# First norm: x turned once without its factor, the factor applied when products are read out; GpSimd splits seven weight units; head sums spaced evenly

## What is computed

```python
n = x * rsqrt(mean(x*x, -1) + eps) * g_mix                # x [512, 1024]
q, k, v, u, bg, cg, ga, gc = split(n @ w_in + b_in)       # 512 x6, 1024 x2
q, k = rms_norm per head of 64, times g_q, g_k
ya = chunked attention(q, k, v) with a bias by distance   # 8 heads
yc = bg * (conv_b + sum_j conv_w[j] * shift(cg * u, j))   # 3 taps
m = sigmoid(ga) * (ya @ w_pa) + sigmoid(gc) * (yc @ w_pc)
h = x + m @ w_o
```

## Time and profile before

| | |
|---|---|
| median of 3 runs | 1943.93 us (1943.56 to 1945.12) |
| the profiled execution | 1943.7 us, of which 1941.5 us from first to last instruction |
| PE busy | 1885.3 us, 97% of the span |
| DVE, ACT, POOL busy | 919.2, 637.9, 139.9 us |
| mean granted TensorE clock | 0.989 |

### The profile page before, as it was taken

The page is one execution under the profiler, slowest core; times in us unless marked ns, Lnnn a source line. Parts: engine busy times, 40 slices in busy tenths (PEclk is TensorE's granted clock), DMA queues, the critical chain, the costliest instruction groups (busy, mean ns, idle before and its releaser), DMA issues.

```text
span 1941.5 us, 31375 instructions
## 1 busy us (share of the span) xinstructions
PE 1885.3 (97%) x13564; PEld 1565.4 (81%) x13564; DVE 919.2 (47%) x1611; ACT 637.9 (33%) x1187; POOL 139.9 (7%) x120
## 2 busy tenths in 40 slices
PE   7999999999999989999899999999999999999998
PEld 6877788866666656669789999998967898888898
DVE  5766334233333333358863423348766564423355
ACT  6344323111111111136432222234466543222242
POOL 0022000110000000000000000005222000000011
PEclk9999999989999999999899999999999999999999
DMA  5222342789999999973112332334311213332343
GB/s 191 88 76 77 110 164 88 280 329 429 430 428 430 428 429 427 428 283 95 56 45 87 90 107 78 97 109 133 110 63 55 87 45 109 99 107 83 102 127 112
DMA packets 57149, 345.16 MB, mean 178 GB/s; under 512 B 7168, under 2 KB 7808, under 8 KB 44976
## 3 DMA queue, kind: packets, MB, share of 16 engines
q1 hardware_dynamic: 53184, 334.15, 46.3%
q0 software_dynamic: 3504, 8.54, 1.2%
q10 hardware_dynamic: 320, 0.43, 0.1%
HBM read 343.09 MB, written 4.19 MB: 179 GB/s over the span
## 4 chain that ended last, share of the span: by engine, by line
PE 87%; DVE 7%; DMA 4%; ACT 1%; issue 1%; POOL 1%; SPq 0%; DVEq 0%; POOLq 0%; ACTq 0%
PE bank L487 57%; PE bank L702 10%; PE bank L726 6%; DMA e<-in_we 3%; PE bank L737 1%; PE bank L738 1%; PE bank L543 1%; PE bank L1135 1%; DVE wlo L1319 1%; PE bank L689 1%; PE bank L919 1%; PE bank L1083 1%; PE bank L880 1%; PE bank L1055 1%; PE bank L560 1%
## 5 line engine op out<-in xcount | busy, mean ns | idle before, releaser
L1319 DVE TENSOR_TENSOR wlo<-raw,whi 128x1024 fp32r<-128x1024 f32 x230 | 288.4, 1261 | 127.2 <-ACT whi L2319 123.5
L2319 ACT CAST whi<-raw 128x1024 fp32r<-128x1024 f32 x231 | 239.8, 1043 | 123.6 <-PE bank L487 106.5
L702 PE MATMUL bank<-e,xT 128*64 128x256 f32 x2048 | 236.9, 385 | 1.1 <-DVE xT L1592 0.8
L702 PEld LDWEIGHTS bank<-e,xT 128*64 128x64 f32 x2048 | 143.6, 138 | 82.5 <-issue 13.0
L487 PE MATMUL bank<-nhi,whi 128*128 128x272 f32 (+1 forms) x672 | 191.6, 285 | 1.1 <-DVE sl L1848 0.6
L487 PE MATMUL bank<-nhi,wlo 128*128 128x272 f32 (+1 forms) x672 | 191.2, 285 | 0.0
L487 PE MATMUL bank<-nlo,whi 128*128 128x272 f32 (+1 forms) x672 | 190.6, 284 | 0.0
L487 PE MATMUL bank<-n1hi,whi 128*128 128x512 f32 (+1 forms) x448 | 162.6, 363 | 0.0
L487 PE MATMUL bank<-n1lo,whi 128*128 128x512 f32 (+1 forms) x448 | 160.7, 359 | 0.0
L487 PE MATMUL bank<-n1hi,wlo 128*128 128x512 f32 (+1 forms) x448 | 160.7, 359 | 0.0
L487 PEld LDWEIGHTS bank<-nhi,whi 128*128 128x128 f32 x672 | 127.2, 189 | 2.0 <-DVE sl L1848 0.8
(11 more groups left out here) (397 smaller groups left out, 3767.9 us busy)
## 6 DMA issues: line engine op xcount, KB each, us to landing
e<-in_we SPq DMA_DIRECT2D x94, 2048.0 KB, 21.2
raw<-in_w_down SPq DMA_DIRECT2D x64, 512.0 KB, 3.5
raw<-in_w_gate SPq DMA_DIRECT2D x44, 512.0 KB, 3.5
raw<-in_w_up SPq DMA_DIRECT2D x44, 512.0 KB, 3.5
raw<-in_w_q SPq DMA_DIRECT2D x12, 512.0 KB, 4.3
B<-in_rel POOLq DMA_DIRECT2D x8, 512.0 KB, 4.9
raw<-in_w_gc SPq DMA_DIRECT2D x8, 512.0 KB, 3.5
raw<-in_w_ga SPq DMA_DIRECT2D x8, 512.0 KB, 4.2
```

What stands on the lines that cost most here:

```text
L702: p = e.matmul(b[64 * hf:64 * hf + 64, 0:256], x[:, k, :], W[:, k, 256 * hf:256 * hf + 256], start=(k == 0), stop=(k == 7))
L1319: e.tensor_tensor(wlo[wslot(u)][:], raw[u % NRAW][:], whi[wslot(u)][:].bitcast(F32), ALU.subtract).then_inc(*hit("dve_low", ("lo", u)))
L2319: e.copy(whi[wslot(u)][:], raw[u % NRAW][:]).then_inc(*hit("act_high", ("hi", u)))
```

## The change

- **Start.** x is turned as it comes. `xhi` and `xlo` are made from the unscaled x. The turned banks are also copied into `hT` (k = 0 and 4 to 7 by ScalarE, 1 to 3 by VectorE), and only that copy frees a bank. `pe_raw_x` goes. SyncE issues weight unit 0 ahead of x. ScalarE casts unit 0 first, squares three tiles, then runs xhi 0, xhi 1, copy 0, xhi 2, xhi 3, the cast of unit 1, xhi 4 to 7, the fourth square, copies 4 to 7.
- **Factor.** The roots are laid on a diagonal (`dg`, one VectorE multiply of two tensors in SBUF). Four fp32 matmuls of ones with it spread them over the partitions (`pe_spread_x`, step 12, in tile q 1), and ScalarE copies them to `rb`.
- **Readout.** Each of q, k, cg, u, bg, gc, ga is multiplied by `rb` on VectorE first: 8 + 12 + 8 + 8 multiplies. For q, k, cg, gc, ga this frees the bank, and ScalarE's bias or sigmoid then works in SBUF. u and bg are multiplied in their bank. V takes the root as the scalar of its one instruction.
- **Units 1 to 7** have their low part made by GpSimd.
- **Head sums** come one per tile: `HEAD_LAG` is 3 for the first and 6 for the others.

The core of the diff:

```diff
+    POOL_LOW = range(1, 8)
...
-                w.wait_ge(*at("xr", i))
+                w.wait_ge(*at("x", i))
...
+        def pe_spread_x():
+            b = take(("rb x",), SIDE)
+            w.wait_ge(*at("diag x"))
+            for i in range(4):
+                p = e.matmul(b[:, i * 128:(i + 1) * 128], ones, dg[:, i, :], start=True, stop=True)
...
-        side.add(nothing(3))
+        side.add(nothing(8))
         side.add(pe_meta())
-        side.add(pe_raw_x(range(6)))
+        side.add(nothing(2))
+        side.add(pe_spread_x())
...
-    HEAD_LAG = 2
+    HEAD_LAG = (3,) + 7 * (6,)
...
         def dve_load():
...
             feed(0)
+            root_x(0)
             for k in range(8):
                 w.wait_ge(*at("x hi", k))
                 e.scalar_tensor_tensor(xlo[:, k, :], bk("x", k), v1("g_mix", k), xhi[:, k, :].bitcast(F32), ALU.mult,
-                                       ALU.subtract).then_inc(*hit("dve_norm", ("xn", k), ("free", "x", k)))
+                                       ALU.subtract).then_inc(*hit("dve_norm", ("xn", k)))
+            for k in (1, 2, 3):
+                e.tensor_copy(hT[:, k, MT:L], bk("x", k)).then_inc(*hit("dve_out", ("free", "x", k)))
+            root_x(2)
+            w.wait_ge(*at("root", "x", 0))
+            w.wait_ge(*at("root", "x", 2))
+            e.tensor_tensor(dg[:], ident.unsqueeze(1).to_broadcast([128, 4, 128]),
+                            xs[:, 0, 0:4].unsqueeze(2).to_broadcast([128, 4, 128]), ALU.mult).then_inc(
+                                *hit("dve_norm", ("diag x",)))
+
+        def x_scaled(to, *key):
+            w.wait_ge(*at("free", "rb x"))
+            w.wait_ge(*at("out", *key))
+            e.tensor_tensor(to, bk(*key, 0), rb[:, 0:S], ALU.mult).then_inc(*hit("dve_out", ("free", *key, 0)))
+
+        def x_scaled_there(*key):
+            w.wait_ge(*at("free", "rb x"))
+            w.wait_ge(*at("out", *key))
+            e.tensor_tensor(bk(*key, 0), bk(*key, 0), rb[:, 0:S], ALU.mult).then_inc(*hit("dve_out"))
+            w.wait_ge(*last("dve_out"))
...
                 tile(J["bg", i], 0, at_k={1: first, 3: lambda: tap(1), 5: lambda: tap(2)})
+                x_scaled_there("bg", i)
...
         def dve_branches():
...
+                tile(J["gc", h], 0, at_k={CONV_LAG: lambda: conv_low(3)} if h == 0 else {})
+                tile(J["gc", h], 1, at_k={1: lambda: gate(0)})
                 for m in range(2):
                     k = 2 * h + m
-                    tile(J["pc", h], m)
-                    w.wait_ge(*at("free", "gc", k, 0))
+                    tile(J["pc", h], m, at_k={} if m else {1: lambda: gate(1)})
+                    w.wait_ge(*at("gate c", k))
...
         for i in range(8):
             tile(J["q" if i < 4 else "k"], i % 4)
-            side.add(nothing(HEAD_LAG))
+            for j in (0, 1) if i == 1 else (i,) if i else ():
+                dve_head(j)
+            side.add(nothing(HEAD_LAG[i]))
             side.add(dve_head_norm(i))
...
         def act_head(i):
             n = "q" if i < 4 else "k"
             z = qk[:, i, :]
-            w.wait_ge(*at("out", n, i % 4))
-            e.activation(z, bk(n, i % 4, 0), ACT.Identity, bias=v1("b_in", i)).then_inc(
-                *hit("act_out", ("free", n, i % 4, 0)))
+            w.wait_ge(*at("free", n, i % 4, 0))
+            e.activation(z, z, ACT.Identity, bias=v1("b_in", i)).then_inc(*hit("act_out"))
...
-        low(1)
+        for u in POOL_LOW:
+            low(u)
...
+        load(0)
         for i in range(4):
             e.dma_start(xt[:, i, :], T["x"][i * 128:(i + 1) * 128, :]).then_inc(*dma(f"d_x{i}", ("x", i)))
```

More of the change, by code:

```diff
@@ L598, in pe_branches @@
             side.drain()
[L600 to L607, removed]
+        def pe_spread_x():
[3 more added lines that the diff above has]
+                p = e.matmul(b[:, i * 128:(i + 1) * 128], ones, dg[:, i, :], start=True, stop=True)
+            p.then_inc(*hit("pe_norm", ("spread x",)))
+            yield
         def pe_mix():
@@ L1328, in tile, with root_x @@
                     side.tick()
+        def root_x(i):
+            y, m, u = (xs[:, n, i:i + 2] for n in range(3))
+            w.wait_ge(*at("x sq", i + 1))
+            e.tensor_scalar(m, m, 1.0 / D, EPS, ALU.mult, ALU.add).then_inc(*hit("dve_mean", ("mean", "x", i)))
+            root(e, w, y, m, u, "dve_root", "x", i)
         def dve_load():
             e.memset(epst[:], EPS).then_inc(*hit("dve_set", ("eps",)))
[L1332 to L1339, removed]
             feed(0)
+            root_x(0)
             for k in range(8):
@@ L1427, in dve_conv @@
                 tile(J["cg", i], 0, at_k={CONV_LAG: lambda: conv_low(i - 1)} if i else {})
-                tile(J["u", i], 0)
-                w.wait_ge(*at("free", "cg", i, 0))
-                w.wait_ge(*at("out", "u", i))
+                tile(J["u", i], 0, at_k={1: factor})
+                x_scaled_there("u", i)
+                w.wait_ge(*at("cg", i))
                 e.scalar_tensor_tensor(z[:, 2:S + 2], bk("u", i, 0), v1("b_in", 12 + i), z[:, 2:S + 2], ALU.add,
@@ L2347, in act_load, with x_copy @@
                     *hit("act_norm", ("x hi", k)))
+            def x_copy(k):
+                w.wait_ge(*at("xn", k))
+                e.copy(hT[:, k, MT:L], bk("x", k)).then_inc(*hit("act_out", ("free", "x", k)))
+            feed(0)
+            for i in range(3):
+                x_square(i)
+            w.wait_ge(*at("vec"))
+            x_high(0)
+            x_high(1)
+            x_copy(0)
+            x_high(2)
+            x_high(3)
+            feed(1)
+            for k in range(4, 8):
+                x_high(k)
+            x_square(3)
+            for k in range(4, 8):
+                x_copy(k)
         def act_head(i):
@@ L2420, in act_branches, with gate @@
                     tile(J["gc", h], m, at_k={CONV_LAG - 1: lambda: conv_high(3)} if k == 0 else {})
[L2421 to L2424, removed]
+                    if m:
+                        gate(k - 1)
                 for m in range(2):
                     tile(J["pc", h], m)
+                    if m == 0:
+                        gate(k)
             side.drain()
[L2429 to L2434, removed]
         def act_mix():
+            def gate(k):
+                z = sg[:, k % 2, :]
+                w.wait_ge(*at("free", "ga", k, 0))
+                e.activation(z, z, ACT.Sigmoid, bias=v1("b_in", 24 + k)).then_inc(*hit("act_out", ("gate a", k)))
             for h in range(4):
@@ L2928, in scalar @@
         act_load()
-        side.add(nothing(4))
-        side.add(act_raw_x(range(6)))
-        side.add(nothing(1))
+        side.add(nothing(13))
         for i in range(8):
             tile(J["q" if i < 4 else "k"], i % 4)
-            act_head(i)
-            side.add(nothing(HEAD_LAG))
+            if i == 1:
+                w.wait_ge(*at("spread x"))
+                e.copy(rb[:, 0:S], bk("rb x")).then_inc(*hit("act_out", ("free", "rb x")))
+            for j in (0, 1) if i == 1 else (i,) if i else ():
+                act_head(j)
+            side.add(nothing(HEAD_LAG[i]))
             side.add(act_head_norm(i))
-            if i == 2:
-                side.add(act_raw_x((6, 7)))
         act_values()
```

77 lines of the change are left out of this document (41 added, 36 removed).

## The result

The changed kernel takes 1961.63 us (median of 6 runs, 1957.09 to 1966.51), the kernel before 1943.57 beside it. The recorded ratio is 1.0085, interval 1.0074 to 1.0095. So it is slower by 16.5 us by the ratio and by 18 by the medians, where 1942.9 and "no change" were forecast. The profiled execution is the slowest of the six, 1966.5 us with a span of 1964.7, so its rows show about 5 us more than the median has.

The account below looks back on a forecast made before the run. TensorE, busy 97% of the span, was taken as the bound, its list of instructions being the time. The sum was 1943.7 - 1.9 - 3.5 + 1.0 + 1.4 + 0.7 + 1.5 = 1942.9 us, range 1939.6 to 1946.8.

Parts of the forecast that it names:

- two signs of being wrong: The forecast is wrong if the roots follow TensorE at 6.4 us, or if the start is not at 14.
- Everything behind w_o hangs on TensorE's progress: After w_o: everything hangs on TensorE or transfers it releases, so earlier gains or losses pass on one to one.
- The start: TensorE's first product comes at 14.2 instead of 16.77 us; less a 0.7 wait for `xlo[4]`, net gain 1.9.
- TensorE's list: Eight turns of unscaled x go, saving 3.5 us; the spread's four fp32 matmuls add 1.0; head sums only move.
- The head norms become a ring: Head stage: ScalarE and VectorE wait on each other, 7.8 us a turn against TensorE's 6.35; cost 1.4, bounds 0 and 3.
- the wait at a head sum: Head stage: once the slack is used up, TensorE waits 1.4 us for `hsq` at head sum 5.
- Behind it come the v units, whose low parts are made by then: After head sum 5: v's low parts are ready and the last two sums find their squares ready; no further wait.
- Attention: Of 12 added multiplies only the one after bg 2 is uncovered: TensorE waits 0.7 us for GpSimd's unit 11 result.
- gc to pc: VectorE frees gc 1's bank late, behind `yalo`; TensorE waits 1.5 us at pc 1, only for h = 0.
- The close race: `dg` on VectorE (23.3) against GpSimd's unit 2 low part (23.4); GpSimd first: TensorE waits 1.7 us, 1944.6, chance 0.18.
- The third rival: Head norms: GpSimd's subtractions also hold up reciprocals, 3.4 to 4.8 us; 1947.0, or 1948.7 if `dg` is held too; chance 0.12.

Follow-up runs that it names:

- e6: The kernel before with its unread filler products ahead of the branch 512 columns wide instead of 256, 36 instructions fewer: 1951.9 us, ratio 1.0045.
- e11: e4 with the router's unread filler products 512 columns wide instead of 256, 24 instructions fewer before TensorE's branch: 1944.1 us, ratio 0.9988.
- e1: The changed kernel with GpSimd making the low part of unit 1 alone, as before the change: 1955.2 us, ratio 1.0059.
- e4: The changed kernel with the edits of e2 and e3 together, and the last head pair's `yalo` three steps later: 1945.4 us, ratio 1.0003.
- e5: e4 with six unread filler products in the router written as twelve half as wide, 24 instructions more: 1938.5 us, ratio 0.9975.
- e7: The changed kernel with only the edit of e5, the twelve narrower unread products in the router: 1956.6 us, ratio 1.0070.
- e10: e5 without the later `yalo`, so made ahead of the multiply that frees gc 1's bank: 1941.3 us, ratio 0.9981.
- e3: The changed kernel with a third `hsq` buffer and VectorE's reciprocal and product of the head norm one tile end later: 1954.6 us, ratio 1.0051.
- e9: e5 with GpSimd's unit 2 subtraction allowed after the second root's mean and unit 3's only after `dg`: 1941.1 us, ratio 0.9983.
- e2: The changed kernel with GpSimd waiting for `dg` before unit 2, still splitting units 1 to 7: 1957.4 us, ratio 1.0068.
- e8: The kernel before with GpSimd splitting units 1 to 7 instead of unit 1, the first norm as it was: 1945.0 us, ratio 1.0005.

## Why the prediction was wrong

**What the stall behind the experts is.** A product in these traces is a weight load and a matmul, two instructions. Counted in the programs, and the same in the traces' records, the place where TensorE goes on behind its overflow branch (it skips the code for extra pairs of experts) lies, against the changed kernel, 4 instructions later in e6 and 24 earlier in e11. The products made before the stall are 3 in the changed kernel (and in e1 to e4, which have its count), 1 and 15. That gives the stall's place as 6, 4 + 2 = 6 and -24 + 30 = 6. It is one fixed place in TensorE's program, and the engine stands there when it comes too soon after the branch: between products 2.5 to 3.1 us (2.6 in the changed kernel) after three, 2.8 after one, 1.45 after fifteen. With the continuation moved past that place (e5 and e7, 24 later; the kernel before has it 40 later) there is no stall. The profile's queues show instructions arriving in transfers of 16 KB (109 of them, 1.79 MB), and one such transfer ends at 884.2 us in the changed kernel, 1.3 us before TensorE goes on. In all seven traces with the stall it goes on 1.3 to 1.4 us after the end of such a transfer. The Trainium skill ("Vector Engine (DVE) Microarchitecture Reference", section "Instruction fetch and dispatch (NX sequencer)") gives an instruction 64 bytes, so by an estimate from that page such a transfer would hold 256 of them. The page is about VectorE; this case's trace agrees as far as it can be asked: TensorE has 27,457 records in the changed kernel, 252 for each of the 109 transfers. That the place is the border of a transfer is what fits all of this. The runs show the fixed place, its removal, and the transfer just ahead of the restart, not the border itself.

**The steps, in the prediction's order.** Neither of its two signs of being wrong came: the roots are 7.7 apart and the start is at 14.5.

- *"Everything behind w_o hangs on TensorE's progress ..., so I pass a gain or loss on one to one."* This failed. The change makes TensorE's program 40 instructions shorter (32 transposes fewer, four fp32 products of two passes and eight waits more: 64 - 16 - 8), and that put the branch's continuation six instructions ahead of the place. The sum had nothing for it, as it took time only from instructions and waits. Cost: 5.0 (e7), 6.9 (e4 to e5), and 8.1 when brought upon the kernel before (e6). In the traces the stage takes 62.4 to 64.8 us in the seven with the stall and 55.7 to 56.7 in the six without it.
- *The start*: first product at 14.5 for 14.2, net gain 1.8 for 1.9. *TensorE's list*: right in sum. The cleanest trace for it is e10's, whose clock stays up until after w_o and which lacks only the ring's wait: it reaches w_o at 329.1, 2.1 ahead, where the sum without the ring has 1.9 + 3.5 - 1.0 - 0.7 - 1.5 = 2.2.
- *The head norms become a ring*: period (7.72 for 7.8) and the wait at a head sum (1.1 for 1.4) right. The step that failed is "Behind it come the v units, whose low parts are made by then". I followed their weights and not their banks. The group of v that takes the bank of k 3 waits 3.6 us for the ring's last multiply, and 6.8 us at half the clock follow. All of the ring costs 7.0 (e3) instead of 1.4.
- *Attention* 0.6 for 0.7, *gc to pc* 1.4 for 1.5 (e10: 1.2 in the time, not clear of noise).
- *The close race* went GpSimd's way, which had 0.18. Its price was the third failed step: 1.7 assumes one instruction held. For one that is about right (e9: a wait of 1.2, 1.6 in the time). But GpSimd began 0.5 sooner than I had it (22.91 for 23.4), when two steps of the root were still to come, and it had three subtractions ready, so that each of the two steps and `dg` was held by one of its own. `dg` was ready at 30.46 instead of 24.0, the wait was 5.3, and it brought the slow stretch. Removing it gives 4.3 (e2) to 6.4 (e1).
- *The clock*: no term of the sum has a fall of it. A wait of 5.3 or 3.6 us costs 2.7 to 2.9 more by the estimate above.
- *The third rival*, that reciprocals are held too, didn't come: they keep 3.35 us, also beside GpSimd. Here the Trainium skill's rule ("SBUF — State Buffer", section "Who interferes with whom") and the traces agree: the reciprocal at 49.15 took 3.35, and held were only instructions with two inputs in SBUF (0.16 to 2.3, 0.69 to 2.79, and in e5 0.75 to 2.08).

Alone, the four removals (e2, e3, e7, and e10's term) give 4.3 + 7.0 + 5.0 + 1.2 = 17.5, together 23.2. The single differences are rough: the intervals of e2 and e7 overlap with the changed kernel's, whose six runs spread over 9.4 us (e5's nine over 2.9). In the traces the two causes of the first stage do add up: at the first scores e2 is 9.2 ahead of the changed kernel, e3 8.5, both together (e4) 17.3. But that stage itself differs between executions: e7, the same program up to the router, comes to its first scores 2.8 earlier, with 1.1 of that at the first product and 3.4 instead of 6.8 us at half the clock behind the wait for k 3. That the missing 5.7 us are such falls of the clock, here or later, is argued, not shown. With all of them gone, e5 is 5.4 us faster than its kernel before; the prediction's sum without the ring's and pc 1's waits is 1942.9 - 1.4 - 1.5 = 1940.0 (unit 11's wait is still there), and it runs 1938.5. I can't assign the 1.5 between them.

## What to carry to other kernels

When an instruction that frees a bank moves from an engine that is ahead to one that works in a ring, look up who takes that bank next, not only who waits in the ring. When two engines can race for SBUF, don't price one collision but as many as the other engine has instructions ready, and let it wait for the short chain to be done: that one wait was worth 4.3 us by the medians. And any edit that changes the number of TensorE's instructions ahead of a branch can move time behind it. A wait "on issue" right behind a branch, in a stage that the edit doesn't touch, is the mark, and a few filler products more are the test and the cure.

## What was unexpected of the hardware

A wait of TensorE costs more than itself once the granted clock falls: behind 5.3, 3.6, and the stall's 2.2 to 2.8 us of waiting it was at half for 6.8 to 13.7 us (3.4 behind the 3.6 of e1 and e7). After 1.2 (e9) and 1.4 us (e10) it stayed up in the profiled execution, while behind e11's idle of 1.2 (1.45 between products) it fell in the profiled one, and it fell for 6.8 us behind a wait of 1.5 ahead of 405.85 in the kernel before. The length of the wait is not all: the one of 2.2 us for GpSimd, which all 13 traces have (ahead of 217.38 in the changed kernel), left the clock up in seven of them, the two given kernels among them, and took it to half for 3.4 us in six (e3 to e8). And the two kernels before (as given, and e6) do the same arithmetic and differ by 8.1 us, 6.7 of them in one stage, through how the filler products ahead of a branch are cut.
